# A paged-attention decoder kernel: the pages of the selected branch loaded from two queues instead of one

## The reference

```python
def _mixer_sample(h, pool_c, pool_s, win_buf, pool_buf, page_table, P):
    q, (kc_, vc_), (ks_, vs_), (kw_, vw_), gates, gu, gv, p = _project(h, w_in, pos)
    def full(pool_kv, k_new, v_new):
        past = pool_kv[page_table].reshape(B, -1, 2, N_KV_HEADS, HEAD_DIM)
        ...
    kfs, vfs = full(pool_s, ks_, vs_)          # selected branch: 8 x 16 pages
    o_c, o_s = _cmp_slc_attend(q, pos, *keys)  # compressed and selected branch
    o_w = _attend(q, kwb, vwb, _win_mask(pos, kpos))   # window branch
    o_nsa = _gate_merge(gates, o_c, o_s, o_w)
```

## Time and profile before

| | us |
|---|---|
| median of 3 runs | 3140.19 (3138.5 to 3151.82) |
| profiled execution | 3141.96 |
| its span in the profile | 3140.4 |
| PE busy | 2699.4 (86%) |
| DVE busy | 1010.3 (32%) |
| ACT busy | 757.3 (24%) |
| POOL busy | 327.2 (10%) |

### The profile page before, as it was taken

How to read it: one execution, slowest core, us unless ns; L and a number is a source line. 1 busy time by engine, 2 the same in 40 slices (tenths; PEclk the granted TensorE clock), 3 DMA queues, 4 the chain that set the end, 5 groups by cost and what they waited for, 6 DMA issues and landing times.

```text
span 3140.4 us, 48600 instructions
## 1 busy us (share of the span) xinstructions
PE 2699.4 (86%) x17740; PEld 2394.5 (76%) x17740; DVE 1010.3 (32%) x1772; ACT 757.3 (24%) x1050; POOL 327.2 (10%) x121
## 2 busy tenths in 40 slices
PE   7999998993577979999889999979846879799995
PEld 7999786982244779999889987869713548799995
DVE  2221213252253452223232212240624435522414
ACT  2221001320132232223132210022201322322322
POOL 0000000420000120003210000013100002200133
PEclk9999999985578889999999999989755889899997
DMA  3223432122221112221222234311322211122221
GB/s 135 81 93 120 135 119 82 56 97 66 94 59 49 41 63 85 91 106 59 80 74 87 90 126 139 125 58 61 110 58 93 58 41 68 60 88 88 83 92 73
DMA packets 134777, 265.54 MB, mean 85 GB/s; under 512 B 15315, under 2 KB 113778, under 8 KB 115314
## 3 DMA queue, kind: packets, MB, share of 16 engines
q1 hardware_dynamic: 132770, 250.01, 23.6%
q0 software_dynamic: 1888, 13.94, 1.2%
HBM read 258.15 MB, written 14.24 MB: 87 GB/s over the span
## 4 chain that ended last, share of the span: by engine, by line
issue 86%; POOL 7%; PE 6%; DVE 1%; DVEq 0%; POOLq 0%; ACT 0%; ACTq 0%
PE PS L448 6%; POOL wo_lo L380 2%; POOL xs L387 2%; POOL wi_lo L433 1%; POOL wi_lo L393 1%; PE PS L594 0%; DVE H L1431 0%; DVEq L1279 0%; DVE H L1282 0%; DVE sm L1398 0%; DVE M L1425 0%; DVE H L1410 0%; DVE PR L1282 0%; ACT H L1019 0%; POOLq L386 0%
## 5 line engine op out<-in xcount | busy, mean ns | idle before, releaser
L448 PE MATMUL PS<-xs,wi_hi 128*128 128x272 f32 x5632 | 1072.3, 290 | 69.7 <-POOL xs L387 43.1
L448 PEld LDWEIGHTS PS<-xs,wi_hi 128*128 128x128 f32 x5632 | 892.9, 190 | 73.9 <-POOL xs L387 46.8
L448 PE MATMUL PS<-xs,wi_lo 128*128 128x272 f32 x3072 | 893.4, 291 | 0.0
L448 PEld LDWEIGHTS PS<-xs,wi_lo 128*128 128x128 f32 x3072 | 585.3, 191 | 0.0
L380 POOL TENSOR_TENSOR wo_lo<-WO,wo_hi 128x2816 fp32r<-128x2816 f32 x28 | 175.7, 6276 | 1777.0 <-ACT wo_hi L1019 1777.0
L448 PE MATMUL PS<-H,WO 128*128 128x272 f32 x1408 | 330.8, 397 | 5.5 <-DMA WO<-wo_dram 4.0
L448 PEld LDWEIGHTS PS<-H,WO 128*128 128x128 f32 x1408 | 268.9, 192 | 66.3 <-issue 11.1
L1282 DVE TENSOR_TENSOR wi_lo<-WI,wi_hi 128x2048 fp32r<-128x2048 f32 x84 | 192.5, 2292 | 387.4 <-ACT wi_hi L1019 387.4
L448 PE MATMUL PS<-wo_hi,xs 128*128 128x352 f32 x960 | 237.8, 327 | 36.0 <-POOL xs L387 29.7
L1019 ACT ACTIVATE wi_hi<-WI 128x2048 fp32r<-128x2048 f32 x89 | 170.4, 1915 | 287.4 <-DMA WI<-wi_dram 287.4
L448 PE MATMUL PS<-h_hi,wo_hi 128*128 128x272 f32 x704 | 205.4, 292 | 9.4 <-DVE h_lo L1282 9.4
(11 more groups left out here) (193 smaller groups left out, 2961.1 us busy)
## 6 DMA issues: line engine op xcount, KB each, us to landing
WI<-wi_dram SPq DMA_DIRECT2D x100, 1024.0 KB, 4.8
WO<-wo_dram SPq DMA_DIRECT2D x44, 1408.0 KB, 6.0
M<-cmp_t_dram SPq DMA_DIRECT2D x256, 128.0 KB, 2.3
M<-slc_k_dram SPq DMA_DIRECT2D x256, 64.0 KB, 1.9
M<-slc_v_dram SPq DMA_DIRECT2D x256, 64.0 KB, 1.8
o_win_s_dram<-win_rows_dram POOLq DMA_DIRECT2D x2, 4064.0 KB, 5.7
M<-win_k_dram SPq DMA_DIRECT2D x2, 2048.0 KB, 8.0
M<-win_v_dram SPq DMA_DIRECT2D x2, 2048.0 KB, 10.0
```

The source lines that it names most:

```text
L448: return nc.tensor.matmul(out, lhsT, rhs, start=start, stop=stop, skip_group_check=True)
```

## The change

The two halves of `CR` get a queue each for the selected branch. SP keeps n = 0 and 2 of the keys and of the values (half 0) and the window loads. n = 1 and 3 of the keys and of the values (half 1) move to POOL, through a new `load_groups` there with the same page-number reads, the same DMA shapes and the same conditions on `cr_freed`. POOL's DMAs count on a new semaphore `pages_late`; `cr_full[1]` keeps the compressed pages and the window values, so its count for each layer shrinks to `CR_DMAS_1`, and PE's waits follow.

In POOL's order, the first load (keys, n = 1) stands behind the `o_pool_p` store and ahead of the other stores of the layer, with a new wait on `wo_done` in front (the one that SP has at L341). Keys n = 3 and values n = 1 and 3 stand behind `o_gv`, ahead of the four subtractions for the output projection.

```diff
-CR_DMAS = 4 * NPG + 1 + 2 * 2 * NPG + 2 * 2 * NPG
+CR_DMAS = 4 * NPG + 1 + 4 * 2 * NPG
+CR_DMAS_1 = 4 * NPG + 1
...
                 def load_groups(first, src):
                     with sp.Fori(0, 2) as a:
-                        for h in range(2):
-                            sp.wait_ge(cr_freed, at(l, NCR, first + 1 + 2 * a + h))
-                            own(sp)
-                            load_half(l, a, h, src)
+                        sp.wait_ge(cr_freed, at(l, NCR, first + 1 + 2 * a))
+                        own(sp)
+                        load_half(l, a, 0, src)
...
+            def load_groups(l, first, src, a):
+
+                pool.wait_ge(cr_freed, at(l, NCR, first + 2 + 2 * a))
+                own(pool)
+                with pool.Fori(0, 4) as j:
+                    pages = nc.values_load_multi_w_load_instructions(
+                        pt_sb[0:1, ds(4 * NPG * a + NPG * j + LOT, LOT)], engines=[mybir.EngineType.Pool],
+                        min_val=0, max_val=NPHYS - 1)[1]
+                    for n, page in enumerate(pages):
+                        pool.dma_start(CR[:, 1, ds((LOT * j + n) * P, P)],
+                                       src[ds(l * NPHYS + page, 1), :, :].rearrange("o p n -> p (o n)")
+                                       ).then_inc(pages_late, 16)
...
                 pool.wait_ge(pj_freed, at(l, 30, 30 + 5))
                 own(pool)
+                pool.wait_ge(wo_done, at(l, NWO, KD + NCH + 2))
+                own(pool)
...
+                load_groups(l, B, slc_k, 0)
...
                 pool.dma_start(lw(o_gv, "o s n -> (o s) n"), pj[0:NS, NT, C_V:C_V + 256]).then_inc(stored, 16)
+                load_groups(l, B, slc_k, 1)
+                for a in range(2):
+                    load_groups(l, B + 6, slc_v, a)
...
-                pe.wait_ge(cr_full[h], 16 * at(l, CR_DMAS, 4 * NPG + 2 * NPG * (a + 1)))
+                if h == 0:
+                    pe.wait_ge(cr_full[0], 16 * at(l, CR_DMAS, 4 * NPG + 2 * NPG * (a + 1)))
+                else:
+                    pe.wait_ge(pages_late, 16 * at(l, 8 * NPG, 2 * NPG * (a + 1)))
```

More of the change, by code:

```diff
@@ L226, in build @@
         cr_full = [sem("cr_full0"), sem("cr_full1")]
+        pages_late = sem("pages_late")
         wi_done, wo_done, cr_freed = sem("wi_done"), sem("wo_done"), sem("cr_freed")
@@ L394, in low_first @@
                                         ALU.subtract).then_inc(first_split, 1)
+            def load_groups(l, first, src, a):
[9 more added lines that the diff above has]
+                                       ).then_inc(pages_late, 16)
             low_first(1)
+            pool.wait_ge(tab_loaded, 16)
+            own(pool)
             with pool.Fori(0, DEPTH) as l:
@@ L649, in beside @@
                     if not after:
-                        pe.wait_ge(cr_full[p], 16 * (at(l, CR_DMAS, NPG) + NPG * i))
+                        pe.wait_ge(cr_full[p], 16 * (at(l, (CR_DMAS, CR_DMAS_1)[p], NPG) + NPG * i))
                     for v in (2 * p, 2 * p + 1):
@@ L741, in win_values @@
                 own(pe)
-                pe.wait_ge(cr_full[1], 16 * at(l, CR_DMAS, 8 * NPG + 1))
+                pe.wait_ge(cr_full[1], 16 * at(l, CR_DMAS_1, 4 * NPG + 1))
                 for a in range(2):
@@ L790, in slc_values @@
                 own(pe)
-                pe.wait_ge(cr_full[h], 16 * at(l, CR_DMAS, 8 * NPG + 1 + 2 * NPG * (a + 1)))
+                if h == 0:
+                    pe.wait_ge(cr_full[0], 16 * at(l, CR_DMAS, 8 * NPG + 1 + 2 * NPG * (a + 1)))
+                else:
+                    pe.wait_ge(pages_late, 16 * at(l, 8 * NPG, 4 * NPG + 2 * NPG * (a + 1)))
                 if h == 0:
```

## The result

| | median of the runs, us | range, us | profiled execution, us | its span, us | PE busy | granted clock |
|---|---|---|---|---|---|---|
| before | 3139.93 (4 runs) | 3138.5 to 3151.82 | 3141.96 | 3140.4 | 86% | 0.894 |
| after | 2999.7 (4 runs) | 2991.49 to 3005.64 | 3005.64 | 3004.1 | 89% | 0.916 |

The ratio is 0.953, with an interval of 0.9503 to 0.9557: 140 us less, where 125 were forecast.

The account below looks back on a forecast made before the run. The prediction took SP's own instructions, a 36 us beat for 32 pages, to bound the kernel. Gains of 52.5, 44.5, 15.8 and 12.4 sum to 125.2; 3140.2 - 125.2 = 3015 us, range 2985 to 3060.

Parts of the forecast that it names:

- What bounds the kernel: Page supply to PE: SP's own instructions set a beat of 36 us for 32 pages, 11 DMA instructions, 25 register work.
- Keys, layer 1: Key pieces of layer 1: scores 3 start at 783.7 instead of 836.2, a gain of 52.5 us.
- Keys, layer 2: Key pieces of layer 2: scores 3 start at 2348.0 instead of 2392.5, a gain of 44.5 us.
- Values, layer 1: Value pieces: waits of 7.13 and 13.40 go, values 1 come 4.7 later; gain 15.8 us, in layer 2 12.4.
- The sign given for it: Page loads on POOL in the changed trace: 32 pages should take 37 to 42 us from first to last.
- What costs nothing: POOL's register reads, later stores and last load, and the window keys: no cost; stores up to 40 us if waited for.
- serial POOL: POOL's page loads: page numbers, issue and writing out without overlap, 61 us a load; 3116 us, chance 0.10.
- the slower case: POOL's page loads: writing out also stands still while DVE works, 77 us a load; 3241 us, chance 0.04.
- DVE held: Value stage: DVE stands still during POOL's writing, 18 us a layer, 36 in all; 3051 us, chance 0.10.
- The in-between case: POOL's page loads: some overlap lost, 50 us a load; 3047 us, chance 0.10.
- Starving: Key loads beside the copy: load 2 and POOL's pages are held, 20 us more a layer; 3055 us, chance 0.04.
- the split does nothing: Page loads on both queues: pages meet in a shared resource behind the queues; 3140 us, chance 0.04.

Follow-up runs that it names:

- all_pool: The changed kernel with both halves of the selected pages on POOL's queue, none on SP; 3177.78 us, ratio 1.0085 to the kernel before.
- before_nocheck: The kernel before, all page loads on SP, without the range check of the page numbers; 3040.94 us, ratio 0.9667.
- copy_late: The changed kernel with the 4 MB copy moved behind POOL's last value load; 2996.65 us, ratio 0.9503 to the kernel before.
- keys_only: The changed kernel with all value loads back on SP, only the key loads split; 3059.92 us, ratio 0.9712 to the kernel before.
- values_only: The changed kernel with all key loads back on SP, only the value loads split; 3101.81 us, ratio 0.9848 to the kernel before.
- best: The changed kernel with the 4 MB copy behind POOL's last value load and no page-number range check; 2976.75 us, ratio 0.9456 to the kernel before.
- before_again: The kernel before, unchanged, run and traced once more; 3142.38 us in its one run.
- slow_pool: The changed kernel with POOL reading each block's page numbers three times; 3127.22 us, ratio 0.9926 to the kernel before.

## Why the prediction was right, and where it was off

The forecast was 3015, in a range of 2985 to 3060; measured were 2999.7. Its steps in order:

- **What bounds the kernel.** Right. all_pool shows that one sequencer gives the beat whatever engine it is on, before_nocheck that fewer register instructions shorten it. The sentence of the Trainium skill weighed there, that issuing from several engines saves a time "which is usually small relative to the DMA itself", is right in its mechanism: that time is what was saved. Its "usually" does not cover 64 KB pages with addresses from a table, where splitting it brought 140 us of 3140.
- **Keys, layer 1.** 52.5 predicted, 51.4 measured. Scores 0 started at 716.85 (716 predicted), the wait at scores 2 was 20.84 (19), scores 3 came without one at 786.10 (783.7). Of these 2.4 us the stage began 1.3 later. SP's load 2 took 48.2 from the freed half to the go (720.5 to 768.7), not 46: the copy's price was 10, not 8.
- **Keys, layer 2.** 44.5 predicted, 45.6 measured. Scores 3 are bound by POOL, with the short wait foretold (2.78 us). Two errors met here: POOL's load was 39.2 us (2231.9 to 2271.1) instead of 42, and the stretch up to scores 1 was 29.7 us instead of the 28.5 used.
- **Values, layer 1.** 15.8 predicted, 23.5 measured; this is the term that was mis-sized, and layer 2 likewise, 12.4 against 24.2. The mechanism was as said: values 2 and 3 lost their waits, values 1 came later. Values 1 were only 0.8 and 1.2 us later, not 4.7, because a load on POOL takes 38.1 and not 42: the upper end was chosen, and the lower one held. That is 3.9 and 3.5 us of the difference. The sign given for it, 37 to 42 us from the first page to the last, was too long as well: it was 32.5 (850.1 to 882.6), and 32.0 on SP in copy_late.
- **Values, what a wait costs besides itself.** The other 3.8 us in layer 1 were no term at all. Take the first 64 matmuls of a value piece, in the changed kernel, behind a wait (n = 1), then without one (n = 2, n = 3), columns as in the earlier trace rows:

```profile
884.60:888.40 3.80, 3.64 (x64) 2.96 (x64) 0.00 (x0) 0.00 (x0) 0.00 (x0) 0.50 0.06 18
911.80:913.80 2.00, 2.00 (x66) 1.69 (x64) 0.00 (x0) 0.35 (x1) 1.44 (x3) 1.00 0.22 66
931.80:933.80 2.00, 1.95 (x65) 1.68 (x64) 1.60 (x6) 1.26 (x3) 0.00 (x0) 1.00 0.03 8
```

Behind the wait of 7.7 us the granted clock is 0.50 (the lower level, 1.2 GHz) and the 64 matmuls take 3.64 us; where PE comes straight from other work it is 1.00 (2.4 GHz) and they take 1.95. In the kernel before, the piece n = 3 stood behind a wait of 13.40 and took 3.64; the stretch is

```profile
1006.30:1010.00 3.70, 3.62 (x64) 2.96 (x64) 0.00 (x0) 0.00 (x0) 0.00 (x0) 0.50 0.02 4
```

How much of the work behind a wait runs at the lower level differs from case to case. From the start of values 2 (its first instruction is a short `PS<-H`, at 970.99 before and at 911.43 now) to the request for values 3 it was 22.0 us in layer 1 and 26.0 in layer 2, and it is 20.4 in both, now that no wait stands ahead of values 2. That is 1.6 and 5.6 us. From values 1 to the request for values 2 it was 29.0 and 29.1, and it is 26.8 and 26.7, though both kernels have a wait ahead of values 1. The piece and the unit behind it, before and after:

```profile
934.80:943.70 8.90, 8.58 (x77) 5.90 (x77) 1.26 (x4) 1.05 (x3) 0.00 (x0) 0.51 0.21 59
884.60:891.30 6.70, 6.39 (x76) 4.76 (x76) 1.26 (x4) 0.67 (x3) 0.00 (x0) 0.68 0.17 49
```

The same work took 8.9 us at 0.51 and 6.7 at 0.68, so these 2.2 us (2.4 in layer 2) are the clock too. But they are not shown to come from the split: the kernel before, traced again, has 29.0 in layer 1 and 27.0 in layer 2, and keys_only, whose values are not split, has 26.8 in both. In before_nocheck, where no wait stands ahead of values 1, the same stretch is 25.0.

The list of waits hides this cost. In the kernel before the page's arrival sets the start of the next piece, so slower work in between only makes the counted wait shorter: 22.0 + 13.4 in layer 1, 26.0 + 9.7 in layer 2. What the late page costs is read from start to start, 35.4 and 35.7 against 20.4. In layer 2 the stretches gained 8.0 us in all, and the first wait there was 6.6 where the forecast took 6.9. values_only shows a surplus of the same size with the keys untouched (12.5 us in both layers), so it belongs to the value stage. The forecast took the time between two pieces from the kernel before, as if it did not depend on the wait ahead of it.

- **What costs nothing.** Mostly as said. The window branch took 60.4 us before the values instead of 61.3. POOL's first subtraction for the output projection still waits for ScalarE and not for POOL's own page loads. It meets DVE's work there in another order than in the first trace of the kernel before, which is no effect of the split (last section).
- **The last stretch.** The forecast had no term for it, and it took 10.5 us more in the profiled execution. The kernel before, run again, has 586.5 where its first profile had 576.9, and best has 576.8 where the changed kernel has 587.4: either value occurs with and without the split. The 20 us of gating and pooling in layer 2 that begin 30 us behind the last value piece are, in the kernel before, before_again, the changed kernel and best (columns as in the earlier trace rows),

```profile
2593.50:2613.50 20.00, 17.74 (x146) 14.37 (x144) 9.36 (x24) 4.26 (x7) 3.29 (x1) 1.00 0.28 106
2584.30:2604.30 20.00, 18.14 (x115) 15.03 (x116) 8.57 (x22) 3.09 (x4) 1.89 (x1) 0.75 0.28 106
2446.70:2466.70 20.00, 18.63 (x119) 15.00 (x118) 8.57 (x22) 3.24 (x5) 3.17 (x1) 0.72 0.27 106
2404.40:2424.40 20.00, 17.64 (x145) 14.08 (x144) 9.35 (x24) 4.60 (x8) 4.50 (x1) 1.00 0.28 106
```

At a granted clock of 1.00 PE got through 146 and 145 matmuls, at 0.75 and 0.72 through 115 and 119. So the 10 us come mostly from the clock, and nothing here ties it to the change. In this pair of traces they hide part of the gain: the stages give 146.8, the spans 136.3. What decides which clock a trace gets there stays open.

The sum of the four terms was 125.2, and 144.7 were measured for the same four. Twelve of the missing 19.5 us are the faster stretches between the value pieces (3.8 and 8.3), 7.4 the shorter load on POOL.

**The rivals.** A serial POOL is out: 38.1 us a load, and slow_pool shows what 58 would have done. So is the slower case, since POOL's DMA instructions beside DVE's work in the value stage were 534 ns in the median and 699 at most. DVE held is out: its busy time as a whole is 1019.8 us, 9.5 more than before, and 8.7 of that are two single instructions in the output projection (last section), not beside POOL's page loads. The in-between case would need a load of 50 us. Starving: SP's load was held back beside the copy for 10 us, POOL's pages of load 3 hardly (33.5 us from first to last issue, 745.0 to 778.5, landing within 6.7). That the split does nothing is refuted by the result.

## What to carry to other kernels

When a consumer starts at a steady beat that its own work does not explain, look at the engine that issues its DMAs: divide the beat by the number of DMAs and compare with the length of one DMA instruction; the remainder is register work (1.1 us a page here, of which the DMA instruction was 0.34), and it can be cut (the range check alone, 107 us) or split over two sequencers (140), together 184. Price a wait on TensorE from start to start of the pieces that it separates, with what the following matmuls lose at the lower clock (1.6 and 5.6 us here behind waits of 7.1 and 7.7), not only with its length. And when one of two alternating suppliers is sped up, look at once at the other: the late copy took 16 us from one wait and 9 came back at the next.

## What the runs showed of the hardware

- **POOL issues pages nearly as fast as SP.** Its DMA instruction is 534 ns against 342, but POOL's sequencer works out the next address meanwhile: the three register instructions between two pages run from 850.10 to 850.39 us, the DMA instruction from 850.12 to 850.66. On SP they stand one behind the other (DMA instruction to 724.17, register instructions from 724.21 to 724.52, next DMA at 724.55). all_pool's last key pieces are 38.2 us apart where SP's are 36. A page from POOL lands 2.1 us after its issue, from SP 1.9.
- **A copy from memory to memory holds back small loads of another queue while the DMA engines are not full on average.** In the stretch from 717 to 738 us the 16 engines are at 0.62 of their time and 244 GB/s (0.83 at most, from 722 to 727), and still one DMA instruction of SP, begun at 732.9, stands for 7.05 us, and a page lands up to 18.7 us after its issue. The share is a mean over the engines; whether single ones were full it doesn't say.
- **One instruction of DVE took 5.09 us instead of 0.72 beside a subtraction on POOL.** In layer 2's output projection (columns as in the earlier trace rows) the changed kernel has

```profile
2478.01 9.54 DVE L1310 TENSOR_TENSOR xs<-M,xs 128x544 fp32r<-128x544 f32 x8 [0.19 <-issue]
2481.76 4.58 POOL L455 TENSOR_TENSOR wi_lo<-WI,wm_hi 128x2048 fp32r<-128x2048 f32 x1 [13.74 <-ACT wm_hi L1047]
```

and the kernel before

```profile
2618.46 5.17 DVE L1282 TENSOR_TENSOR xs<-M,xs 128x544 fp32r<-128x544 f32 x8 [0.19 <-issue]
2622.73 5.36 POOL L433 TENSOR_TENSOR wi_lo<-WI,wm_hi 128x2048 fp32r<-128x2048 f32 x1 [8.03 <-ACT wm_hi L1019]
```

In the first, seven of DVE's eight take 0.71 to 0.73 us, and the one that began at 2481.84, 0.08 us behind POOL's, takes 5.09, POOL's whole 4.58 and its own time. In the second none of DVE's is held, and POOL's takes 5.36. In layer 1 of the kernel before POOL's began at 1075.54, 0.08 us ahead of a DVE instruction too, but there POOL's took 5.90 and no DVE instruction more than 0.73. So one of the two stands while the other works, and the recorded starts do not tell which. The split does not decide it: the kernel before, traced again, has DVE held in both layers, in layer 2 with

```profile
2616.90 9.54 DVE L1282 TENSOR_TENSOR xs<-M,xs 128x544 fp32r<-128x544 f32 x8 [0.19 <-issue]
2620.65 4.58 POOL L433 TENSOR_TENSOR wi_lo<-WI,wm_hi 128x2048 fp32r<-128x2048 f32 x1 [13.75 <-ACT wm_hi L1019]
```

and keys_only in neither. The Trainium skill, "SBUF — State Buffer", section "SBUF: two separate sides", says that a DVE instruction with two SBUF inputs and a GpSimd instruction that reads SBUF exclude each other for a whole instruction; these rows agree with it.
- **The granted clock of a stretch is not the same in every run of one kernel.** From scores 0 to scores 1 one trace of the changed kernel took 20.8 us in layer 1 and 29.7 in layer 2, another 20.7 and 25.9. From values 1 to the request for values 2 one trace of the kernel before has 29.0 in layer 1 and 27.0 in layer 2, and its last stretch is 576.9 or 586.5. Two single traces that differ by 10 us in a stretch say nothing on a change until the clocks of that stretch are compared.
